# Both halves of the split weights 64 bytes later in SBUF, and the vectors' rows laid over a later buffer

## The reference

```
for layer in range(4):
    h = rms_norm(x, norm_w[layer])                  # (512, 1024)
    proj = h @ w_in                                 # 1024 x 4096, 10240, 3072 or 4096
    y = mixer(proj) * gate                          # small matmuls, elementwise work
    x = x + y @ w_out                               # 1024 x 1024
```

## Time and profile before

| what | before |
|---|---|
| median of 3 runs | 1349.05 us (1348.72 to 1349.2) |
| span of the profiled execution | 1346.8 us |
| TensorE busy | 1339.1 us, 99%, 8759 matmul records |
| weight loads busy | 1118.0 us, 83% |
| VectorE busy | 923.1 us, 69% |
| ScalarE busy | 687.2 us, 51% |
| GpSimd busy | 145.3 us, 11% |
| DMA | 113.62 MB, mean 84 GB/s |
| mean granted TensorE clock | 1.000 |

### The profile page before, as it was taken

The page is one execution under the profiler, slowest core; times in us unless marked ns, Lnnn a source line. Parts: engine busy times, 40 slices in busy tenths (PEclk is TensorE's granted clock), DMA queues, the critical chain, the costliest instruction groups (busy, mean ns, idle before and its releaser), DMA issues.

```text
span 1346.8 us, 22178 instructions
## 1 busy us (share of the span) xinstructions
PE 1339.1 (99%) x8759; PEld 1118.0 (83%) x8759; DVE 923.1 (69%) x1659; ACT 687.2 (51%) x1226; POOL 145.3 (11%) x224
## 2 busy tenths in 40 slices
PE   9999999999999999999999999999999999999999
PEld 8888888888888888888888887788888888888887
DVE  7867778564767576666676676865657577777782
ACT  6445555353655565656565656553434335454550
POOL 2422333000000000000000000000000022332220
DMA  6322233423222222222223131332333322232221
GB/s 194 95 80 79 64 94 95 118 79 91 66 79 79 79 79 79 79 79 79 79 68 90 48 92 50 105 93 71 94 94 94 110 76 83 63 93 76 84 64 63
DMA packets 211688, 113.62 MB, mean 84 GB/s; under 512 B 3743, under 2 KB 209889, under 8 KB 211586
## 3 DMA queue, kind: packets, MB, share of 16 engines
q1 hardware_dynamic: 211202, 112.02, 28.9%
q0 software_dynamic: 384, 0.20, 0.1%
HBM read 110.10 MB, written 2.10 MB: 83 GB/s over the span
## 4 chain that ended last, share of the span: by engine, by line
PE 96%; DVE 2%; ACT 1%; issue 1%; DMA 0%; SPq 0%; ACTq 0%; DVEq 0%
PE ps L647 39%; PE ps L662 38%; PE scores L662 4%; PE ps L1088 2%; PE ps L1072 2%; PE ps L1028 2%; PE ps L881 1%; PE scores L1056 1%; PE ps L1056 1%; PE scores L852 1%; PE ps L676 1%; PE ps L883 1%; PE scores L870 1%; PE scores L819 1%; PE ps L892 1%
## 5 line engine op out<-in xcount | busy, mean ns | idle before, releaser
L647 PE MATMUL ps<-op_hi,w_hi 128*128 128x512 f32 (+1 forms) x800 | 311.7, 390 | 0.0
L647 PE MATMUL ps<-op_lo,w_hi 128*128 128x512 f32 (+1 forms) x800 | 305.4, 382 | 0.0
L647 PE MATMUL ps<-op_hi,w_lo 128*128 128x512 f32 (+1 forms) x800 | 304.5, 381 | 0.0
L662 PE MATMUL ps<-w_hi,op_hi 128*128 128x512 f32 (+1 forms) x728 | 294.0, 404 | 1.6 <-DVE op_lo L1844 1.6
L662 PE MATMUL ps<-w_lo,op_hi 128*128 128x512 f32 (+1 forms) x728 | 282.6, 388 | 0.0
L662 PE MATMUL ps<-w_hi,op_lo 128*128 128x512 f32 (+1 forms) x728 | 282.2, 388 | 0.0
L1786 DVE TENSOR_TENSOR w_lo<-raw,w_hi 128x1024 fp32r<-128x1024 f32 x200 | 245.1, 1251 | 12.4 <-ACT w_hi L1274 10.9
L1274 ACT ACTIVATE w_hi<-raw 128x1024 fp32r<-128x1024 f32 x200 | 203.0, 1052 | 26.8 <-PE ps L662 11.2
L647 PEld LDWEIGHTS ps<-op_lo,w_hi 128*128 128x128 f32 x800 | 150.4, 188 | 29.9
L647 PEld LDWEIGHTS ps<-op_hi,w_hi 128*128 128x128 f32 x800 | 150.5, 188 | 27.4 <-DVE op_lo L1829 0.2
L647 PEld LDWEIGHTS ps<-op_hi,w_lo 128*128 128x128 f32 x800 | 150.7, 188 | 27.0
(11 more groups left out here) (228 smaller groups left out, 1944.9 us busy)
## 6 DMA issues: line engine op xcount, KB each, us to landing
raw<-in_b_w_in SPq DMA_DIRECT2D x80, 512.0 KB, 3.9
raw<-in_a_w_in SPq DMA_DIRECT2D x64, 512.0 KB, 4.2
raw<-in_c_w_in SPq DMA_DIRECT2D x24, 512.0 KB, 4.1
raw<-in_a_w_out SPq DMA_DIRECT2D x16, 512.0 KB, 4.3
raw<-in_b_w_out SPq DMA_DIRECT2D x8, 512.0 KB, 4.0
raw<-in_c_w_out SPq DMA_DIRECT2D x8, 512.0 KB, 4.9
xt<-in_x SPq DMA_DIRECT2D x4, 512.0 KB, 6.2
y<-in_norm_w SPq DMA_DIRECT2D x3, 512.0 KB, 4.7
```

The lines of the kernel that those rows point to most:

```text
L647: last = nc.tensor.matmul(bank, a, b, start=(k == 0 and p == 0), stop=(k == KT - 1 and p == 2))
L662: last = nc.tensor.matmul(bank, a, b, start=(k == 0 and p == 0), stop=(k == KT - 1 and p == 2))
```

## The change

`w_hi` gets a tensor that is 16 elements (64 bytes) longer, and the view that the kernel uses begins behind these. So `w_hi`, and `w_lo` behind it, lie 64 bytes later; `xt`, `op_hi`, `op_lo`, `y` and `raw` in front of them stay. `vec_rows` no longer has memory of its own but is the first 128 columns of `a_sq` in 40 partitions. Everything after `w_lo` up to `eps` moves 64 bytes up, and everything behind the old `vec_rows` moves 448 bytes down.

```
-        w_hi = sb("w_hi", [P, SLOTS, KT, P], F32R)
+        w_hi = sb("w_hi", [P, 16 + SLOTS * KT * P], F32R)[:, 16:].rearrange("p (s k c) -> p s k c", s=SLOTS, k=KT)
         w_lo = sb("w_lo", [P, SLOTS, KT, P], F32R)
...
-        vec_rows = sb("vec_rows", [40, P])
         vec = sb("vec", [P, 40])
...
         a_sq, at = carve(at, TT, P)
+        vec_rows = a_sq[0:40, 0]
...
-                    nc.tensor.transpose(spare[:, 0:40], vec_rows[:], ident[0:40, 0:40]).then_inc(s_vecT, 1)
+                    nc.tensor.transpose(spare[:, 0:40], vec_rows, ident[0:40, 0:40]).then_inc(s_vecT, 1)
```

## The result

The changed kernel takes 1363.1 us (median of 3 runs, 1362.76 to 1363.11) against 1349.05, a ratio of 1.0105 with a 95% interval of 1.0087 to 1.0123. It is slower by 14 us; the forecast was 1371, slower by 22. The profiled execution has a span of 1360.9 us against 1346.8.

What follows compares the result with a forecast made beforehand. The prediction took TensorE's pace through its own matmuls as the bound. Its terms, 21.5 + 2.0 - 1.6 = +21.9 us, on 1349.05 gave 1371 us, +1.6%; the range holding 8 in 10 was 1346 to 1381.

Steps and rivals of the forecast that it cites:

- likeliest case: Lines 647 and 662 both slower at 512 columns: 1371 us, own range 1362 to 1380, chance 0.60 for slower everywhere.
- What bounds the kernel: Whole kernel: TensorE, busy 1339.1 of 1346.8 us, sets the end; the change adds nothing to its list and removes nothing.
- The `e_op` stretch: Matmuls against `e_op`, already 64 bytes from `w`: 233.3 against 226.7 ns, so +6.67 ns per 512-wide matmul; itself unchanged.
- Settled: 512-wide matmuls of lines 647 and 662 at steady 226 or 227 ns spacing: 3217 x 6.67 ns = +21.5 us.
- The one-way rival: Only line 647, moving operand 64 bytes before the stationary one, slows; line 662 is neutral: +9 us, 1358 us, chance 0.11.
- Unsettled: 986 512-wide distances soon after other matmuls, mean 231.3 ns, would come to 233.3: +2.0 us.
- 256 wide: 240 matmuls of 256 columns with `w` and `op` each gain 6.67 ns: -1.6 us.
- Seams: Places where TensorE changes from one kind of matmul to another or the next one waits: 0 us.
- The vectors' rows: `vec_rows` sharing memory with `a_sq`: rows are dead 40 us before the first write there, 0 us.
- the splits: 200 on VectorE and as many ScalarE copies, writing 64 bytes off their reads: at worst 2.2 us of VectorE, covered, so 0.
- Faster: 512-wide matmuls of lines 647 and 662 settle at 220.0 ns: gain of 23 us, 1326 us, chance 0.21.

## Why the prediction was right, and where it was off

The measured 1363.1 us lies in the range, but that alone says little: 1346 to 1381 also holds no change at all. The likeliest case's own range began at 1362, just below what was measured, and no term of the sum gives that floor (the settled ones and the 256-wide ones alone are 1349 + 21.5 - 1.6 = 1369); that this range holds the result is in part luck. What bears the forecast out is the mechanism, term by term.

*What bounds the kernel, and that nothing but the spacing changes.* Right. The chain is TensorE to 96% in both, the longest waits are the same within 0.1 us, the busy times of VectorE and ScalarE within 0.5.

*The `e_op` stretch as the measure of 64 bytes.* Right for line 647, in sign and to 0.1 ns: 2061 distances with a mean of 233.3. The offset, not `e_op` or its time, is the cause: the kernel with the offset and the one with both operands moved show it, and so does the `e_op` stretch once it is aligned (227.3). One reading on the way was wrong: the stretch was said to have less work of VectorE beside it than the fast one, but 5.41 of 11.10 us is 49% and 2.36 of 5.40 is 44%. Only ScalarE and DMA had less to do there. The argument did not hang on it, and the aligned versions answer it. The rule of the Trainium skill that was weighed against the row, in "TensorE: Matmul & The Clock Gate" under "Step-by-step: what each phase is for" (two independent read ports), gives no change, and 14 us of change were measured; whether a read conflict is the mechanism is not shown by any run here.

*Settled, 3217 x 6.67 = +21.5 us.* This is the term that was mis-sized. It took the price of one sign for both. Line 647's share, 10.6 of the 21.5, came as +11.6 with its unsettled ones in it. Line 662's share was put at 10.8 and measured +3.9: there the moving operand is 64 bytes behind, its long runs settle at 229 ns (+2.3), all but the one of 96 that follows directly on line 647's even 233.3 and keeps it. With its part of the unsettled ones the forecast had charged line 662 some 11.8 us, which is 7.9 too many and more than accounts for the whole error of 7.8 (21.9 against 14.1). The one-way rival had named this gap in the rows, and had priced the other sign at 0 in place of +3.9 us; its 1358 us is 5 below the time measured, the forecast's 1371 is 8 above. The truth is between the two cases.

*Unsettled, +2.0 us.* It was a charge on top of both lines' settled ones. In line 647 it fits: after the change all its distances average 233.3, and 11.6 is 10.6 and 1.0 of this. In line 662 nothing of it can be told apart from the mean of 229.6.

*256 wide, -1.6 us.* The sign was right, the size smaller: -1.1. Line 647's settled at 113.3 ns as forecast; the 48 of line 662, with the other sign, came to 117.8. And the statement that the `e_op` stretch stays as it is was wrong at 256 columns (+0.3 us), where there are two patterns again, 113.3 and 117.8, at the same distance between the operands. In the kernel with everything moved the stretch is back at its old mean with the operands in the very same places, so what else ran decides.

*Seams at 0.* They took +0.7 us, most of it (0.6) in the 198 first distances behind other matmuls. The other matmuls took 1.3 us less; that has no explanation here.

*The vectors' rows, the splits: 0.* Right; the kernel with the alias alone is at 1.0001, and the split on VectorE takes 1253 in place of 1251 ns.

*The rivals.* "Faster" had asked whether another pattern is stable at the same offset. One is, at +64, but it lies at 228.9 ns, above 226.7, and none of the 27 offsets tried within 256 bytes goes below.

## What to carry to other kernels

When TensorE is 99% busy, read the distance between the starts of neighbouring matmuls, not their duration, and look in the kernel's own trace for a stretch whose operands happen to lie at another offset: it prices a move of a buffer before it is made. Then ask for which of the two operands and which sign that stretch speaks; this forecast's error came almost whole from the line whose sign no row showed. In a kernel like this one, of back-to-back float32r matmuls with 512 columns and a weight load each, keep moving and stationary operands at the same place modulo 256 bytes, all halves of them; for narrower ones measure, since 256 and 448 columns had their best elsewhere.

## What the hardware showed that was not expected

- The spacing of back-to-back float32r matmuls hangs on the difference of the two operands' places modulo 256 bytes: 226.7 ns at 0, 228.9 to 237.5 at the others tried, at a granted clock of 1.00. The multiples of 64 are +64: 228.9, +128: 232 to 233, +192: 233.3.
- It is not symmetric. Behind the four transposes +64 and -64 settle 4.4 ns apart (228.9 and 233.3).
- At +64 two patterns are stable, 228.9 and 233.3 ns. What ran before has a part in the choice: a stretch of -64 that went 233, 233, 234 handed its 233.3 on, one that went 236, 231 did not. 256-wide matmuls 64 bytes apart have 113.3 and 117.8, at either sign.
- With only the low half of the weights out of place the kernel loses 15.5 us (1363.74 - 1348.22), with both halves 14; the intervals of the two ratios overlap, so the two are not told apart.
